# The k steps of a feature tile, cut into pieces between the head tokens' small products

## The reference

```python
h = rmsnorm(x, n1)
z = h @ w_in                                   # [u | q | f | i | gate]
y_pool, pool_new = pool_mix(z[..., :D_POOL], pool_prev, pool_start, w_pool, pool_scale)
y_rec, S_new = hgrn2_mix(z[..., D_POOL:], S0, lb, g_norm, lead)
x = x + jnp.concatenate([y_pool, y_rec], axis=-1) @ w_out
y_ffn, conv_new = conv_ffn(rmsnorm(x, n2), conv_prev, w_a, w_b, conv_w, conv_b, w_down)
```

## Time and profile before

| | us |
|---|---|
| median of 3 runs | 2571.3 |
| lowest and highest run | 2568.69, 2573.85 |
| span of the profiled execution | 2573.1 |
| PE busy | 2489.9 (97%) |
| DVE busy | 1207.3 (47%) |
| ACT busy | 717.0 (28%) |
| POOL busy | 449.7 (17%) |

### The profile page before, as it was taken

The page is one execution under the profiler, slowest core; times in us unless marked ns, Lnnn a source line. Parts: engine busy times, 40 slices in busy tenths (PEclk is TensorE's granted clock), DMA queues, the critical chain, the costliest instruction groups (busy, mean ns, idle before and its releaser), DMA issues.

```text
span 2573.1 us, 36513 instructions
## 1 busy us (share of the span) xinstructions
PE 2489.9 (97%) x13263; PEld 2109.4 (82%) x13263; DVE 1207.3 (47%) x2297; ACT 717.0 (28%) x1457; POOL 449.7 (17%) x331
## 2 busy tenths in 40 slices
PE   7898999999999999999999999999999999999997
PEld 7778789999777888888887888888887887888886
DVE  6968465333346864221246774221236774321234
ACT  4214232222223332111233342211233342211133
POOL 4526246555550110000000020000000020000000
PEclk9979999999999999999999999999999999999999
DMA  7641357776757424555656423555655623455653
GB/s 250 215 149 51 125 199 267 249 261 249 278 211 268 156 87 165 191 192 183 237 196 227 183 83 131 213 191 185 235 196 196 231 99 131 180 191 184 234 201 134
DMA packets 145350, 489.03 MB, mean 190 GB/s; under 512 B 8881, under 2 KB 79778, under 8 KB 96025
## 3 DMA queue, kind: packets, MB, share of 16 engines
q1 hardware_dynamic: 136747, 482.58, 52.0%
q10 hardware_dynamic: 8472, 4.75, 0.6%
HBM read 375.45 MB, written 112.02 MB: 189 GB/s over the span
## 4 chain that ended last, share of the span: by engine, by line
PE 88%; DVE 6%; issue 2%; DMA 2%; ACT 1%; POOL 1%; SPq 0%; DVEq 0%; ACTq 0%
PE ps L567 23%; PE ps L569 23%; PE ps L568 22%; PE ps L633 11%; PE ps L788 3%; PE ps L614 1%; PE ps L813 1%; DMA w_both<-w_split 1%; PE ps L820 1%; POOL w_both L543 0%; DVE arena L2022 0%; PE ps L926 0%; PE ps L598 0%; DVE arena L1838 0%; DVE arena L2054 0%
## 5 line engine op out<-in xcount | busy, mean ns | idle before, releaser
L567 PE MATMUL ps<-h_hi,w_both 128*128 128x512 f32 (+1 forms) x1536 | 586.8, 382 | 3.1 <-issue 3.1
L569 PE MATMUL ps<-h_lo,w_both 128*128 128x512 f32 (+1 forms) x1536 | 583.2, 380 | 0.0
L568 PE MATMUL ps<-h_hi,w_both 128*128 128x512 f32 (+1 forms) x1536 | 579.5, 377 | 0.0
L568 PEld LDWEIGHTS ps<-h_hi,w_both 128*128 128x128 f32 x1536 | 288.8, 188 | 58.9
L569 PEld LDWEIGHTS ps<-h_lo,w_both 128*128 128x128 f32 x1536 | 288.3, 188 | 59.5
L567 PEld LDWEIGHTS ps<-h_hi,w_both 128*128 128x128 f32 x1536 | 288.2, 188 | 59.0 <-issue 4.0
L567 PE MATMUL ps<-w_both,act_hi 128*128 128x512 f32 (+1 forms) x748 | 297.4, 398 | 2.0 <-DVE x_tok L2136 1.8
L569 PE MATMUL ps<-w_both,act_hi 128*128 128x512 f32 (+1 forms) x748 | 296.2, 396 | 0.0
L568 PE MATMUL ps<-w_both,act_lo 128*128 128x512 f32 (+1 forms) x748 | 295.4, 395 | 0.0
L2213 DVE TENSOR_TENSOR act_lo<-arena,act_hi 128x512 fp32r<-128x512 f32 (+1 forms) x176 | 139.2, 793 | 328.3 <-ACT act_hi L1527 327.9
L633 PE MATMUL ps<-h_hi,w_both 128*128 128x304 f32 (+1 forms) x1664 | 288.7, 296 | 2.0 <-ACT arena L1333 0.8
(11 more groups left out here) (252 smaller groups left out, 3284.2 us busy)
## 6 DMA issues: line engine op xcount, KB each, us to landing
w_both<-w_split SPq DMA_DIRECT2D x288, 1024.0 KB, 4.8
w_split<-w_both SPq DMA_DIRECT2D x96, 1024.0 KB, 6.2
w_raw<-in_w_down SPq DMA_DIRECT2D x24, 512.0 KB, 4.3
w_raw<-in_w_a SPq DMA_DIRECT2D x22, 512.0 KB, 4.2
w_raw<-in_w_b SPq DMA_DIRECT2D x22, 512.0 KB, 4.2
w_raw<-in_w_in SPq DMA_DIRECT2D x20, 512.0 KB, 4.5
x_tok<-in_x_prompt SPq DMA_DIRECT2D x16, 512.0 KB, 7.0
arena<-in_x_prompt SPq DMA_DIRECT2D x16, 512.0 KB, 6.9
```

Source lines behind the costliest of these rows:

```text
L567: nc.tensor.matmul(out, lhs[0], rhs[0], start=first, stop=False)
L568: nc.tensor.matmul(out, lhs[1], rhs[0], start=False, stop=False)
L569: return nc.tensor.matmul(out, lhs[0], rhs[1], start=False, stop=last)
```

## The change

`wide_part` does some of the k steps of a wide feature tile. In `head_attention` the whole tile is replaced by five calls: steps 0 to 3 where the tile stood, step 4 behind the small products, steps 5 and 6 behind the first and second state product, step 7 behind the last transposition. The last head's gate tile is unit 16 = `U_U` + 4, so it goes the same way.

```diff
+            def wide_part(u, banks, ks):
+                s, w = u % 4, wslot(u % 4, KD)
+                pieces = ((ps[:, banks[0], 0:CUT], FRONT), (ps[:, banks[1], HEAD:CUT], BACK))
+                if 0 in ks:
+                    weights(0, u, s, u // 4)
+                for k in ks:
+                    for n, (lhs, rhs) in enumerate(((w[0], h_hi), (w[1], h_hi), (w[0], h_lo))):
+                        for out, cols in pieces:
+                            last = nc.tensor.matmul(out, lhs[:, k, :], rhs[:, k, cols], start=(k, n) == (0, 0),
+                                                    stop=(k, n) == (KD - 1, 2))
+                if KD - 1 in ks:
+                    last.then_inc(unit_done, 1)
...
-                    if h + 1 < HEADS:
-                        pe.wait_ge(u_taken, h + 1)
-                        feature_tile(0, U_U + h + 1, (6, 7))
-                    else:
-                        gate_tile(0, 1, 0)
+                    between = U_U + h + 1
+                    pe.wait_ge(u_taken, h + 1)
+                    wide_part(between, (6, 7), range(0, 4))
                     pe.wait_ge(hat_ready, h + 1)
...
                     last.then_inc(hof_done, 1)
+                    wide_part(between, (6, 7), range(4, 5))
                     pe.wait_ge(hkdt_ready, h + 1)
...
                         last = nc.tensor.matmul(ps[:, 1 + n0 // 4, 0:m * P], kd_tok[0:HEAD, 0, :],
                                                 v_seq[n0 // 4][0:HEAD, :, :], start=True, stop=True)
+                        if n0 < 8:
+                            wide_part(between, (6, 7), range(5 + n0 // 4, 6 + n0 // 4))
                     last.then_inc(hs_done, 1)
                     pe.wait_ge(hof_ready, h + 1)
                     nc.tensor.transpose(ps[0:HEAD, 4, 0:P], o_feat, ident).then_inc(ho_done, 1)
+                    wide_part(between, (6, 7), range(7, 8))
```

## The result

| | before | changed |
|---|---|---|
| median of 9 runs, us | 2568.69 | 2577.38 |
| lowest and highest | 2561.2, 2573.85 | 2567.5, 2583.31 |
| ratio, 95% interval | | 1.0033, 1.0021 to 1.0045 |
| profiled execution, us (span) | (2573.1) | 2581.32 (2579.5) |

The account below looks back on a forecast made before the run. TensorE, busy 97% of the span, was taken as the bound. Terms of +1.3, 0, -1.1 and -0.7 summed to -0.5 us: 2570.8, rounded to 2571 us, range 2564 to 2578.

Parts of the forecast that it names:

- Term 2: TensorE's clock in the head tokens' attention: one fall per head, low spells of 6.8 us, loss as before: 0.
- term 1: Feature tile cut up: 0.08 us for each of 4 further pieces in 4 heads, +1.3 us.
- rival B: Head attention: longer low spells, as state products and single steps don't lift the clock: +8.5 us, total 2579.3; chance 0.13.
- Term 3: Eighth step behind the transposition: fills TensorE's idle time of 2.31 us in the last head, 1.1 us saved.
- Term 4: TensorE's waits for the copied u tile, 0.8 us in three heads: 0.7 us saved.
- Term 5: Masked scores needed earlier, covered by only four steps: wait up to 0.8 us at full clock, none in the forecast.
- Terms 6 and 7: Last head's gate tile in the same pieces: nothing; weights released up to 9 us later, covered by GpSimd's idle time: zero.

Follow-up runs that it names:

- e3: The changed kernel with state products 128 rows deep, rows 48 to 127 set to zero: 2564.54 us, ratio 0.9986 against the kernel before.
- e6: The changed kernel without the eight 4-column products of each head, so outputs are incomplete: 2563.84 us, ratio 0.9982 against the kernel before.
- e9: The changed kernel without the 4-column products and with state products 128 rows deep (zero rows), read for durations: a single execution, 2560.45 us.
- e1: Against the changed kernel, steps 0 to 6 in one run where the tile stood, only step 7 behind the last transposition: 2564.08 us, ratio 0.9987 to the kernel before.
- e8: The changed kernel with steps 4 to 6 moved among the 4-column products and state products 128 rows deep: 2563.11 us, ratio 0.9973 against the kernel before.
- e13: Against the changed kernel, steps 4 to 7 in one run behind the small products, none late: 2576.68 us, ratio 1.0033 to the kernel before.
- e15: Against the changed kernel, steps 0 to 5 in place, 6 behind the fourth 4-column product, 7 late: 2568.07 us, ratio 0.9999 to the kernel before.
- e5: The changed kernel with steps 4, 5, 6 behind the second, fourth, sixth 4-column products, state products uncut: 2563.50 us, ratio 0.9975 against the kernel before.
- e4: The kernel before with state products 128 rows deep (zero rows): 2568.78 us, ratio 0.9994 against the kernel before.

## Why the prediction was wrong

*Term 2, where the clock goes, put at 0, failed.* I took "one fall per head, spells of 6.8 us, and the loss as before". One fall per head was right. The spells were not: they lasted 10 to 13.5 us, and (1-c)T went up by 8.0 us. Some 3 of these lie in loads that were themselves exposed at half clock (half of term 1's 6.5 us), so about 5 us are lost column-bound work, an estimate. The bound was there (rival B, +8.5), with its mechanism: the trio doesn't lift the clock and single steps between its products don't either. e3 shows the part of the shallow depth by taking only that away, e6 that the 4-column products start the fall. I gave B 0.13, because the second head of before came up early; that row showed scores and steps behind the trio, not what stands between its products.

*Term 1, the pieces, was mis-sized:* 1.3 us forecast, bounds 0 to 2.6; measured some 6.5. In the first head steps 4 to 6 took 1.70 us instead of 1.40 and the three state products 4.75 (2.01 + 2.01 + 0.73) instead of 3.81: 1.8 us, a little less in the others, where the first piece ran at full clock. I had priced a piece by a step that followed attention's 128-row products, 0.08 us, and the weights here change between 128 and 48 rows. Nearest by place was not nearest by kind. e9 against e6 puts one change of depth at 0.19 us at full clock.

So the two terms failed by about 5 us each. That rival B's total, +8.0 with the -0.5 of the other terms, comes near the measured +8.7 is in part luck: it had all of it in the clock and steps of 1.40 us.

*Term 3, the late step,* did what it was to do in the last head (the wait fell from 2.31 to 0.94 us), and I missed a larger effect: e1, which has only the late step, gained 4.5 us. That it stands as strong work between the trio and the weak scores is my reading of why, not shown by itself.

*Term 4* was right: PE no longer waits for the u copies anywhere in the changed kernel's head attention. *Term 5* was right for this kernel (no wait for masked scores). Its bound of 0.8 us at full clock was not: such waits were 0.6 us in e3 and e8 and 2.6 in e13. *Terms 6 and 7* were right: GpSimd's last split before the exponents came at 176.59 instead of 162.18 us, and its idle time behind them shrank, but still stood at

```profile
200.53 0.73 POOL L385 TENSOR_TENSOR arena<-arena 128x256 f32<-128x256 f32 x1 [17.54 <-DVE arena L2038]
```

against the earlier trace rows, and PE never waited for it here.

Sum with measured sizes: 6.5 + 5 - (2.31 - 0.94) - 0.8 = +9.3 us; the first transposition of the u rows came at 190.01 instead of 181.29, +8.7, so 0.6 us are left, within the rounding of the shares. That the medians moved by 8.7 as well is a coincidence: the two profiled spans, 2579.5 and 2573.1, differ by 6.4. Of the 2.3 us between, some 1.6 are the kernel before's 3.20 us at half clock from 298.00, where the changed kernel's profile stays at 1.00 from 298 to 320.

Open: why four steps behind the small products (e13) bring longer executions than three with a late one beyond the waits counted above, and why one cut among them (e15) gains nothing where three do. The falls come at other places in the heads from run to run, and one profile of each kernel doesn't settle that. Whether the clock answers to the rows that a product reads, or to something that goes with them, is open too: depth is what was varied.

## What to carry to other kernels

Price a piece of work by the rows of what will stand beside it: where products of shallow and of full depth alternate, each change shows a weight load that a run of one kind hides. What held TensorE's clock in this kernel was full-depth work in three cuts among the products that bring it down (e5, e8), and a step between the last weak products and the next ones (e1); what cost was such work between shallow products or alone behind the small ones. Where shallow products must alternate with deep ones, zero rows that fill them up to 128 were worth 13 us here. Once the clock holds, ask which engine is next: in e8 PE's waits for DVE rose from 2.3 to 5.8 us.

## What the runs showed of the hardware

- Depth counts for the clock, not only columns. The trio of 48 rows stayed at 0.50 with PE wholly busy, and the next tile began low; with 128 rows and the same columns, the three tiles read behind it in e4 ran at 1.00 throughout.
- A change of weight depth costs 0.19 us at full clock (e6 against e9) and 0.3 at half (1.70 against 1.40 us a step), with the load starting together with its own matmul.
- Small products of 4 to 32 columns, 2.24 us without a gap, came ahead of a fall in every head of the kernel before and of the changed one, and in three of four heads of e4, where the state products are deep; without the sixteen records of 4 columns the clock stayed up until PE waited for DVE. Their 2.24 us at full clock became 4.47 at half (e13).
- With PE almost wholly busy, the low spells behind the first three heads' small products lasted some 3.5 us in e3, 6.6 in the kernel before and 10 to 13.4 in the changed one.
